# Differential attention head by head between halves of projection units, with norm weights multiplied into the weights on GpSimd

## The reference, cut to what matters

```python
def shared_kv(h, kv_norm, w_kv):                       # h: output of the first MLP of the second block
    kv = rms_norm(h, kv_norm) @ w_kv                   # [512, 2048]: keys, then values
# diff_attn_mixer on rms_norm(h, b_norm_pre), the same h:
    q = (h @ w_q).reshape(B, S, DIFF_HEADS, 2, DIFF_HEAD_DIM)      # 8 heads, 2 maps of 64
# for every head, 128 queries at a time:
    logits = einsum(q, k) * scale + bias[rel_bucket(k_pos - q_pos)]
    p = softmax(where(allowed, logits, NEG_INF))
    attn = p[:, :, 0] - lam * p[:, :, 1]
    o = rms_norm(attn @ v, subln_w) * (1.0 - lam_init)
# mix = o.reshape(B, S, D) @ w_out;  h = h + rms_norm(mix, b_norm_post)
```

## Time and profile before

| engine | busy us | share of the span |
|---|---|---|
| PE | 2104.4 | 96% |
| PE weight load | 1729.1 | 79% |
| DVE | 1056.7 | 48% |
| ACT | 830.8 | 38% |
| POOL | 230.9 | 10% |

### The profile page before, as it was taken

The page is one execution under the profiler, slowest core; times in us unless marked ns, Lnnn a source line. Parts: engine busy times, 40 slices in busy tenths (PEclk is TensorE's granted clock), DMA queues, the critical chain, the costliest instruction groups (busy, mean ns, idle before and its releaser), DMA issues.

```text
span 2200.3 us, 26781 instructions
## 1 busy us (share of the span) xinstructions
PE 2104.4 (96%) x10717; PEld 1729.1 (79%) x10717; DVE 1056.7 (48%) x1761; ACT 830.8 (38%) x1521; POOL 230.9 (10%) x313
## 2 busy tenths in 40 slices
PE   6999999999999999899999999999899879999998
PEld 5887556888887877788887888888687568888887
DVE  5332846565555353665665433333523736334334
ACT  3154845353333233423334322322522944223222
POOL 8200000010000000223322000000200111000000
PEclk9999999999999999999999999999999989999999
DMA  5435511323332222222112233222323002322222
GB/s 133 101 96 98 70 39 58 115 68 98 100 100 94 100 85 76 97 67 77 58 58 77 89 100 101 104 96 96 105 96 134 20 24 95 103 96 96 96 96 77
DMA packets 163129, 191.98 MB, mean 87 GB/s; under 512 B 22866, under 2 KB 133757, under 8 KB 163005
## 3 DMA queue, kind: packets, MB, share of 16 engines
q1 hardware_dynamic: 158560, 176.15, 25.2%
q0 software_dynamic: 3904, 13.97, 3.4%
q10 hardware_dynamic: 541, 0.15, 0.0%
HBM read 182.91 MB, written 7.34 MB: 86 GB/s over the span
## 4 chain that ended last, share of the span: by engine, by line
PE 89%; DVE 4%; ACT 3%; issue 1%; POOL 1%; DMA 1%; ACTq 0%; SPq 0%; POOLq 0%; DVEq 0%
PE bank L2295 27%; PE bank L2146 12%; PE bank L2148 12%; PE bank L2147 12%; PE bank L2703 2%; PE bank L2215 1%; PE bank L2738 1%; PE bank L2740 1%; PE bank L2739 1%; PE bank L2216 1%; PE bank L2217 1%; PE bank L2432 1%; PE bank L2418 1%; PE bank L2444 1%; DVE PB L1747 1%
## 5 line engine op out<-in xcount | busy, mean ns | idle before, releaser
L1450 DVE TENSOR_TENSOR WHL<-raw,WHL 128x1024 fp32r<-128x1024 f32 x312 | 390.0, 1251 | 574.9 <-ACT WHL L884 574.8
L884 ACT ACTIVATE WHL<-raw 128x1024 fp32r<-128x1024 f32 x312 | 328.4, 1054 | 573.6 <-PE bank L2295 369.2
L2146 PE MATMUL bank<-HXh,WHL 128*128 128x512 f32 x1120 | 440.5, 393 | 3.1 <-ACT BIG L1041 1.6
L2148 PE MATMUL bank<-HXh,WHL 128*128 128x512 f32 x1120 | 437.5, 391 | 0.0
L2295 PE MATMUL bank<-WHL,HXh 128*128 128x512 f32 x1504 | 405.5, 391 | 3.2 <-DVE HXl L1459 2.0
L2147 PE MATMUL bank<-HXl,WHL 128*128 128x512 f32 x928 | 361.6, 390 | 0.0
L2295 PEld LDWEIGHTS bank<-WHL,HXh 128*128 128x128 f32 x1504 | 282.8, 189 | 64.4 <-issue 4.5
L2146 PEld LDWEIGHTS bank<-HXh,WHL 128*128 128x128 f32 x1120 | 211.3, 189 | 48.2 <-issue 3.8
L2148 PEld LDWEIGHTS bank<-HXh,WHL 128*128 128x128 f32 x1120 | 211.1, 188 | 44.5
L2295 PE MATMUL bank<-WHL,HXl 128*128 128x512 f32 x752 | 232.2, 390 | 0.0
L2147 PEld LDWEIGHTS bank<-HXl,WHL 128*128 128x128 f32 x928 | 174.6, 188 | 35.5
(11 more groups left out here) (330 smaller groups left out, 3082.8 us busy)
## 6 DMA issues: line engine op xcount, KB each, us to landing
raw<-in_mlp_w_up_dram SPq DMA_DIRECT2D x64, 512.0 KB, 4.6
raw<-in_mlp_w_down_dram SPq DMA_DIRECT2D x64, 512.0 KB, 4.3
raw<-in_w_up_dram SPq DMA_DIRECT2D x44, 512.0 KB, 5.1
raw<-in_a_w_in_dram SPq DMA_DIRECT2D x32, 512.0 KB, 4.5
raw<-in_w_in_dram SPq DMA_DIRECT2D x24, 512.0 KB, 4.8
raw<-in_w_down_dram SPq DMA_DIRECT2D x22, 512.0 KB, 4.3
raw<-in_w_kv_dram SPq DMA_DIRECT2D x16, 512.0 KB, 4.9
rel_dram<-GB POOLq DMA_DIRECT2D x1, 5120.0 KB, 54.0
```

What stands on the lines that cost most here:

```text
L884: return a.activation(dst, src, ACT.Copy, **k)
L1450: v.tensor_tensor(dst(1), src, dst(0).bitcast(F32), ALU.subtract).then_inc(w_lo, 1)
L2146: m.matmul(b[:, :], w[0][:, k, :], x[0][:, k, :], start=(k == 0), stop=False)
L2148: return m.matmul(b[:, :], w[1][:, k, :], x[0][:, k, :], start=False, stop=(k == KD - 1))
```

## The change

1. **Norm weights on GpSimd.** Norm 5 writes the normed rows once, without a weight (`c = 0 if n == 5`, scale 1.0); HX2h and HX2l are no longer written by it. The 24 units of keys, values and queries are multiplied in place by the norm's weights on GpSimd (`scaled(u)`, a multiply of 128x1024 with the gains broadcast), and ScalarE's split waits for that.
2. **The border by halves.** "down0" gets the form of the other borders: `border(4)`, `norm_halves(5)`, 5 in `HALVES`. GpSimd multiplies units 0 and 1 before the residual, units 2 and 3 between its third and fourth root.
3. **Order of the projections.** Slots are now kq0, dv0, kq1, kq2, dv1, kq3: a kq slot holds the key features and the query features of one head (a unit each); kq0 to kq3 serve two heads each, dv0 and dv1 four each. kq0 is what `norm_halves(5)` runs.
4. **Attention head by head.** `kv_dense(d)` is half a unit, 12 matmuls; 40 of them stand between the pieces of the heads, from `D_AT`. Score pieces use one pair of banks (SC), turns one bank (TURN), outputs one bank (OUT). "d_out" is laid out in blocks and run by `out_product`, its first ones between the steps of heads 6 and 7. The bias masters are loaded two for each head.
5. **The start.** ScalarE issues one row DMA; the other 17 are issued by SP behind the second weight slot; PE turns them behind the first two units. GpSimd's 13 loads stand behind its four norm roots.

```diff
-HALVES = (1, 3, 4, 6)
-NEXT = ("kv01", "up", "ple_gate", "qf0", "up0", "dk", "up1")
+HALVES = (1, 3, 4, 5, 6)
+NEXT = ("kv01", "up", "ple_gate", "qf0", "up0", "kq0", "up1")
+        SC, TURN, OUT = (bank[5], bank[7]), bank[1], bank[3]
+        D_AT = ((8, 14), (14, 20), (20, 26), (26, 31), (31, 36), (36, 40))
...
@@ SP
-                if n == 1:
-                    sp.wait_ge(rows_in, 16 * N_ROWS)
+                if n == RAW:
+                    row_tables()
                 if n >= RAW:
                     sp.wait_ge(*slot_free[n - RAW])
...
@@ GpSimd
+            def scaled(u):
+                n, j = units[unit_at["kq0", 0] + u]
+                pool.wait_ge(ring_full[place(n)], full_after[n])
...
+                g.tensor_tensor(w, w, cols[:, c:c + nk].unsqueeze(2).to_broadcast([P, nk, D // nk]),
+                                ALU.mult).then_inc(w_scaled, 1)
...
                 y_root(2)
                 if not halves:
                     norm_tile(r + 1, 1)
+                if r == 4:
+                    scaled(2)
+                    scaled(3)
                 y_root(3)
...
             resid(3)
+            pool.wait_ge(cols_ready, 2)
+            scaled(0)
+            scaled(1)
             resid(4)
...
+            bias_in(0)
+            scaled(4)
+            scaled(5)
+            for h in range(1, 4):
+                bias_in(h)
+                scaled(4 + 2 * h)
+                scaled(5 + 2 * h)
+            u = 12
+            for h in range(HH + 1):
+                if h:
+                    map_stats(h - 1)
+                for _ in range((3, 3, 3, 2, 1)[h] if h < 5 else 0):
+                    scaled(u)
+                    u += 1
+                if h < 4:
+                    bias_in(4 + h)
@@ ScalarE, split
-                    act.wait_ge(ring_full[place(units[u][0])], full_after[units[u][0]])
+                    if slots[units[u][0]][0][:2] in ("kq", "dv"):
+                        act.wait_ge(w_scaled, u - unit_at["kq0", 0] + 1)
+                    else:
+                        act.wait_ge(ring_full[place(units[u][0])], full_after[units[u][0]])
@@ VectorE, border
                     half_low(n, 0)
-                    split(w + 2)
+                    if r != 4:
+                        split(w + 2)
                     y_gained(r, 3)
                     x_added(r, 3)
+                    split(w + 2)
                     norm_tile(n, 2)
@@ PE
             mlp(0)
-            norm(5)
-            split_features("dk", 8, 5)
-            split_blocks("dv")
+            norm_halves(5)
...
+            map_scores(0, 0)
+            kv_dense(0)
+            map_scores(0, 1)
+            kv_dense(1)
             map_scores(0, 2)
+            for d in range(2, 8):
+                kv_dense(d)
+            for h in range(HH - 2):
+                for i in range(3):
+                    map_scores(h + 1, i)
+                    if i == 2 and h:
+                        map_out_turn(h - 1)
+                    dense_step(h, i)
+                for i in range(3):
+                    turn_map(h, i)
+                    dense_step(h, 3 + i)
+                map_values(h)
+            map_scores(7, 0)
+            out_product(0, name="d_out")
+            map_scores(7, 1)
+            out_product(1, name="d_out")
+            map_scores(7, 2)
+            map_out_turn(5)
+            turn_map(6, 0)
+            out_product(2, name="d_out")
+            turn_map(6, 1)
+            turn_map(6, 2)
+            map_values(6)
+            turn_map(7, 0)
+            out_product(3, name="d_out")
+            turn_map(7, 1)
+            map_out_turn(6)
+            out_product(4, name="d_out")
+            turn_map(7, 2)
+            map_values(7)
+            out_product(5, name="d_out")
+            out_product(6, name="d_out")
...
```

More of the change, by code:

```diff
@@ L1352, in turned_map, with map_exp @@
[L1352 to L1358 removed]
+            border(4)
+            def map_exp(h, i):
+                n = 4 * U_DIFF + 8 * h + (0, 2, 6)[i]
+                for x in range(2):
+                    for qt in PIECES[i]:
+                        n += 1
+                        act.wait_ge(p_biased, n)
+                        s = map_buf(h, x)[:, QOFF[qt]:QOFF[qt] + P * (qt + 1)]
+                        a.activation(s, s, ACT.Exp, bias=amin[:, h % 3, x, qt:qt + 1], scale=-1.0,
+                                     accum_out=asum[:, h % 3, x, qt:qt + 1]).then_inc(p_exp, 1)
@@ new lines, in kv_out, with map_x_high @@
+            def kv_out(d):
+                if d is not None and d % 2:
+                    name, u = DENSE_KV[d // 8], d // 2 % 4
+                    if name[:2] == "kq":
+                        key_query(name, u)
+                    split(unit_at["dv0", 0] + d // 2 + HL)
+            def map_x_high(k):
+                act.wait_ge(ot_evac, HH + k + 1)
+                if k == 0:
+                    act.wait_ge(ps_full, GT["kq3"][0] + 4)
+                copy(HXh[:, k, :], dQ[:, k, :]).then_inc(x_hi, 1)
@@ L1379, in _ @@
-            for h in range(HH + 4):
-                if h >= 3 and h - 3 < HH:
-                    act.wait_ge(ot_psum, HH + h - 2)
-                    copy(dQ[:, h - 3, :], bank[6 + (h - 3) % 2][:, :]).then_inc(ot_evac, 1)
-                if 1 <= h <= HH:
-                    turned_map(h - 1)
-                if h + 1 < HH:
-                    exp_maps(h + 1)
-                if 1 <= h <= HH:
-                    map_squares(h - 1)
-            rows_split("d_out", dQ, lambda k: (ot_evac, HH + k + 1))
+            for i in range(4):
+                key_query("kq0", i)
+                if i >= 2:
+                    split(unit_at["dv0", 0] + i - 1)
@@ new lines, in _ @@
+            w = unit_at["d_out", 0]
+            for i in range(3):
+                map_exp(7, i)
+            map_out_evac(5)
+            map_evac(6, 0)
+            map_evac(6, 1)
+            map_x_high(4)
+            split(w + 3)
+            map_x_high(5)
+            map_squares(6)
+            map_evac(7, 0)
+            split(w + 4)
+            map_evac(7, 1)
+            map_out_evac(6)
+            map_x_high(6)
+            map_squares(7)
+            split(w + 5)
+            map_out_evac(7)
@@ L1390, in _ @@
+            map_x_high(7)
+            split(w + 7)
+            split(unit_at["up1", 0] + 1)
             border(5)
@@ L2096, in _, with kv_low, map_x_low @@
+            def kv_low(d):
+                if d is not None and d % 2:
+                    split(w0 + d // 2 + 2)
+            def map_x_low(k):
+                vec.wait_ge(x_hi, x0["d_out"] + k + 1)
+                v.tensor_tensor(HXl[:, k, :], dQ[:, k, :], HXh[:, k, :].bitcast(F32), ALU.subtract).then_inc(x_lo, 1)
+            split(w0 + 1)
             vec.wait_ge(act_lam, 1)
             chain(v.tensor_scalar(lam[:, 4:5], lam[:, 3:4], lam[:, 2:3], -LAM_INIT, ALU.subtract, ALU.add))
-            chain.settle()
@@ new lines, in _ @@
+            for i in range(3):
+                biased_maps(0, i)
+            kv_low(1)
+            kv_low(3)
+            joined(0)
+            kv_low(5)
+            kv_low(7)
+            values_evac(0, range(TT))
+            for h in range(HH - 2):
+                bias_ready(h + 1)
+                for i in range(3):
+                    biased_maps(h + 1, i)
+                    if i == 0 and h == 4:
+                        values_evac(1, (2, 3))
+                    if i == 1 and h:
+                        gated_map(h - 1)
+                    kv_low(dense_at(h, i))
+                for i in (3, 4, 5):
+                    kv_low(dense_at(h, i))
+                turned_map(h)
+                joined(h + 1)
+                if h == 3:
+                    values_evac(1, (0, 1))
@@ new lines, in _ @@
+            w = unit_at["d_out", 0]
+            map_x_low(0)
+            map_x_low(1)
+            bias_ready(7)
+            biased_maps(7, 0)
+            biased_maps(7, 1)
+            gated_map(5)
+            map_x_low(2)
+            biased_maps(7, 2)
+            map_x_low(3)
+            turned_map(6)
+            joined(7)
+            map_x_low(4)
+            split(w + 3)
+            map_x_low(5)
+            gated_map(6)
+            split(w + 4)
+            turned_map(7)
+            map_x_low(6)
@@ L2112, in _ @@
+            gated_map(7)
+            split(w + 5)
+            map_x_low(7)
+            split(w + 7)
+            split(unit_at["up1", 0] + 1)
             border(5)
@@ L2904, in _ @@
+            for tt in range(TT):
+                if tt == TT - 1:
+                    turn_tile(6, 0)
+                for k in range(KD + 2, 2 * KD):
+                    out_product(k, (tt,), "d_out")
             mlp(1)
```

473 lines of the change are left out of this document (243 added, 230 removed).

## The result

The changed kernel takes 2174.36 us (median of 4 runs, 2171.69 to 2175.14); the kernel before, run beside it on the same chip, 2202.3 (2192.75 to 2204.92). The ratio is 0.9875, with a 95% interval of 0.9859 to 0.9891. A second timing on another chip gave 0.9872 [0.9855, 0.9888]. So the change wins 27.5 us of 2202, where 19.0 were forecast. The sign, the mechanism and the range were right; the size was a third too small. The median lies only 0.4 us inside the fast end of the narrower range, 2174 to 2190.

A forecast was written before the change was run, and what follows sets the result against it. PE held 89% of the chain of waits, so only its idle or low-clock time could be won. Start 5 + border 5.6 + attention 8.4 = 19.0 off 2202.0, less 0.8: 2182 us; range 2167 to 2199, own range 2174 to 2190.

The forecast's parts named there:

- Start: Program start: ScalarE free about 8 us sooner, feature copies at 18.1 instead of 21.85 or sooner; 5 us won, between 0 and 8.
- the rule that the prediction quotes: Start: DMAs of all issuing engines share 16 engines, so spreading them saves issue time alone; the landing stays, 3.7 us won.
- Border: First MLP's down projection to key projection: going by token halves cuts a loss of 11.6 us to 6; 5.6 won.
- Unit 2: First border: VectorE's split of this key/query unit follows the last residual addition, so PE gets it 1.7 us late.
- Attention: Differential attention and its exit: half units between the steps cut a loss of 26.4 us to 18; 8.4 won.
- Insertions, 8.4: Attention: 42 insertions each cost a start, 0.1 us ahead of the scores and 0.11 behind; 8.4 us lost, lower bound 0.
- Missing steps, 3.6, and the end, 4: Attention: three heads lack half units before the values, 3.6 us (0 to 6); chains in heads 7 and 8, 4 (2.4 to 10).
- Locks, 2: Attention: GpSimd and VectorE block each other on shared SBUF ports; 2 us lost, between 0 and 15.
- The rival of complete cover: All three parts: cover as complete as in the recurrence, 32.8 us won (8 + 9.2 + 15.6), 2169 us; chance 0.18.
- The locks' rival: Attention: VectorE meets running GpSimd multiplies at splits or the map subtraction, delaying score pieces, 12 us; 2194 us; chance 0.18.
- GpSimd's pace: Attention: GpSimd's multiplies set the pace from 7.8 us per unit; at 9.5 us the kernel takes 2218 us; chance 0.06.
- That the moved parts do nothing: Start and first border: slot lands later, multiplies hold the border as long as now; 5 + 5.6 fall away, 2193 us; chance 0.08.

The follow-up runs named there:

- the other profile of the old attention: Kernel before with only the new start: 2192.46 us, ratio 0.9978; its attention stage takes 233.9 us in the profile instead of 236.5.
- The two new orders: Changed kernel with half units of heads 3 to 5 placed otherwise, 2167.32 us; changed kernel with the output products at the end reordered, 2165.61 us.
- kernel with both edits: Changed kernel with half units of heads 3 to 5 placed otherwise and the end reordered: 2163.99 us, ratio 0.9827.
- the two experiments on them: Kernel before with the new start alone, 2192.46 us, ratio 0.9978; changed kernel with the first border by whole tiles again, 2182.23 us, ratio 0.992.
- the new layout of banks without it: Changed kernel with all half units put ahead, none between the steps of the heads: 2221.03 us, ratio 1.0099.
- only the bare steps moved: Changed kernel with half units of heads 3 to 5 placed so the step behind the third score piece is bare: 2167.32 us, ratio 0.9852.

## Why the prediction was right, and where it was too small

- **Start**, forecast 5: measured alone 4.8 (1.3 to 8.4), in the profiles 3.6 to 9.3 and 5.7 in the mean. Right. What I had as the likeliest case, a landing at about 16 us, did not come: the slot's second DMA lands at 12.9 us, 9.4 after its issue, where before it landed at 16.8, 13.3 after. With the landing of before, and 1.9 us from there to the first copy, the copies would start at 18.7, 3.1 us sooner; they start 7.0 sooner, and the other 3.9 are the landing. So by the rule that the prediction quotes the landing would have stayed, and here it moved. Which of the transfers taken away from beside it did that, no run separates.
- **Border**, forecast 5.6: measured 8.4. The loss that stays was put at 6. With 114 matmuls at 0.2267 us and 32 transposes at 0.12, the stage holds 12.0 us of loss before and 3.6 after. (The forecast's 11.6 took 27 matmuls as the border's; three of them lie at the window's ends and belong outside.) Two terms fail. Unit 2 comes 0.18 us late and not 1.7. I had taken VectorE's order from the border behind the output projection. Counted from the first transpose, the last addition ends 12.9 us later there (1835.11 to 1848.04) and 11.5 here: no weight split stands ahead of it, and the low halves take 2.74 us where the gain no longer has to be multiplied in. And the 2 us for locks are not there, since PE waits just as long without the multiplies. That I priced a multiply at 3.1 us, scaling the 1571 ns of 128x512 by its elements, where 1.97 were measured, decided nothing.
- **Attention**, forecast 8.4: measured 14.7, or 12.0 against the other profile of the old attention. The forecast was a loss of 26.4 before less 18 after. With the same 7.34 us per head, and 654 full matmuls at the 0.2267 us by which they follow each other in the keys before, this stage holds 29.5 us of loss before (26.8 in the other profile) and 14.8 after.
  - Before, 3.1 were missed. 1.8 are two waits in the stretch ahead of the attention, shown below, into which I had not looked. The rest is within what the clock changes from one profile to the other.
  - Insertions, 8.4: the failing step. A whole head with six of them takes 23.64, and 7.34 + 6 x 2.72 are 23.7, so their net cost is nothing. From one instruction's start to the next, the twelve matmuls of a half unit take 2.88 us in that head, 0.16 more than the 2.72 of a dense stretch: close to the 0.2 that I had priced. But the head's own instructions take 6.34 us and not 7.34. The sum added the price of a start to a busy time that holds such starts already. I had named 0 as the lower bound, and had taken the upper one.
  - Missing steps, 3.6, and the end, 4: too small together. The two new orders give back 10.7 and still leave 3.5 us of waits, the first head's 0.9 among them: 14.2 of the 14.8. One reason is in the windows above: behind waits of 1.7 and 2.2 us PE ran at clock 0.6. I had priced no clock at the missing steps; the 1.6 that I had at the end is what it cost there, but not the waits beside it.
  - Locks, 2: nothing measurable, as the kernel without multiplies shows.

That the total came within the range is partly luck: in the attention, 8.4 us too much for the insertions and 2 for the locks stood against 7.2 too little for the missing steps, the end and the first head. The 3.1 not seen before came on top of that difference.

Three of the signs named did not come as named: the feature copies start at 14.87 and not at 16 to 18, a multiply takes 1.97 us and not 3.1, and the clock, 0.99 over the border and the attention together, is 0.96 over its end. PE idles 9.8 us between the first scores and the output projection's end, under the limit of 15.

Two waits of PE in the kernel before, ahead of its attention:

```profile
1619.75 0.47 PE L2274 MATMUL bank<-WHL,HXh 128*128 128x512 f32 x1 [0.73 <-issue]
...
1664.58 0.47 PE L2146 MATMUL bank<-HX2h,WHL 128*128 128x512 f32 x1 [1.03 <-DVE BIG L2031]
```

The rival of complete cover (2169) had 8 + 9.2 + 15.6 for the three stages; measured are 7.2 + 8.4 + 14.7. In sizes it was the better forecast. As a mechanism it holds in the border and in the middle of the attention (23.64 of 23.64 us), not in heads 4 to 8; its attention term fits because before lost more than I had counted and the insertions cost nothing net. The kernel with both edits, 2164, comes closest to what it describes. The locks' rival (2194) is refuted: the mechanism is there, but the subtraction meets no multiply and the splits have time. GpSimd's pace is a real limit, somewhere between twice and four times the multiply's length. That the moved parts do nothing is refuted by the two experiments on them.

## What to carry to other kernels

When three engines are each near their limit in a chain, put independent matmuls of PE between the steps of that chain: here the order is worth 45 us, while the new layout of banks without it is slower than the old one. Then look for the steps that got none; it is cheaper to leave bare a step whose successor is far than the one whose reader stands right behind it. Time both kernels in more than one profile before a term of a few microseconds is read off: the old attention differed by 2.7 us between two. And before pricing "one more start per insertion", subtract what the starts already cost in the busy time that the sum is built on.

## What the runs showed that was not expected

- GpSimd's multiply of 128x1024 by eight gains broadcast over 128 elements each takes 1.89 us at least and 1.97 in the mean; that of 128x512 with a broadcast takes 1.57. Twice the elements cost a quarter more.
- The split of 6.62 us began at 1571.87, within the first pair of multiplies, which ended at 1572.6. Between this pair and the next GpSimd issued two DMAs for 1.1 us, and the split didn't get through in that gap: it ended at 1578.49, about 1.1 us after the second pair. GpSimd was issuing the next two DMAs just then (1577.34, 1.11 us), so a DMA issue does not by itself keep a split out. Why the first gap was lost is open.
- PE's granted clock fell behind waits of 1.7 and 2.2 us in the last heads of the changed kernel, and not behind those of 0.6. In the kernel with both edits, where no wait of the attention is over 0.9 us, it stays at 1.00. The wait alone does not decide it: with only the bare steps moved, the same 2.2 us wait has clock 1.00 behind it.
